# Four routing passes in place of six over streamed weights, with one buffer of normed rows and a front paced by TensorE time

## The chip, the cores and the metric

One core of a Trainium2 chip runs the whole program. Its engines are TensorE (PE: matmuls, PEld: weight loads), VectorE (DVE), ScalarE (ACT), GpSimd (POOL) and SyncE (SP, which here only issues DMAs); 16 DMA engines move data between HBM and the on-chip memory. The metric is the time of one execution in microseconds (us); lower is better.

## The reference, cut to what matters

One layer of a streaming encoder for 1024 prompt rows and 32 sample rows of width 1024, in float32. After two mixers (a gated linear attention and a forgetting attention, "fox", whose keys and values come partly from a cache) each row picks single-neuron experts by product keys and adds their outputs:

```python
def peer(h, w_q, subkeys, u_tab, v_tab):        # h: (rows, 1024)
    q = (xb @ w_q).reshape(blk, PEER_HEADS, 2, PEER_DKEY // 2)          # 8 heads, 2 halves of 128
    s = jnp.einsum('nhcd,hckd->nhck', q, subkeys)                       # 128 scores per half
    s1, i1 = lax.top_k(s[:, :, 0], 16)
    s2, i2 = lax.top_k(s[:, :, 1], 16)
    cand = (s1[..., :, None] + s2[..., None, :]).reshape(blk, 8, 256)
    top, ti = lax.top_k(cand, 16)
    idx = e1 * 128 + e2                                                 # one of 16384 experts
    g = jax.nn.softmax(top, axis=-1)
    a = jax.nn.gelu(jnp.einsum('nhkd,nd->nhk', u_tab[idx], xb))
    return jnp.einsum('nhk,nhkd->nd', g * a, v_tab[idx])
...
x = x + concat[GLA, FoX] @ w_out
x = x + peer(rmsnorm(x, g_norm2), ...)
```

So each row needs 8 heads x 16 = 128 experts, each with a row of `u` and a row of `v` (4 KB + 4 KB).

## The kernel before, in words

Rows are worked on in tiles of 128: tiles 0 to 7 are the prompt, tile 8 (`TILES`) holds four copies of the 32 sample rows, so that its 128 experts per row take only 32 gathers. The first phase (`mix_phase`, not touched) computes the projections and the linear attention of all tiles. The second, `merged_phase`, is written as two streams that every engine interleaves in the same order:

- the **back** goes through NS = 1056 slots. In slot s GpSimd gathers one expert per row, 128 rows of 8 KB (`u` and `v` together), into a ring of 8 buffers (L983). VectorE forms the dot products of the `u` half with the normed rows `h2` (L1493). A pair of slots makes a group: ScalarE applies the gelu to its two columns (L1102), VectorE multiplies by the routing weights (L1485), and the two `v` halves are added up. An add runs either on TensorE, as two matmuls of 512 columns with a diagonal matrix that ScalarE builds (L1110, L1295; the trace has four records for one add), or on VectorE as one instruction on `sums` (L1501). `on_vector(g)` says how many of a group's two adds VectorE takes: 1 in every odd group, 0 in every even group, so every fourth add. A ring buffer is free for the next gather when its add is done. At the start of a tile `reopen` (L1467) computes `h2` of the tile anew from x_mid rows that GpSimd's queue has loaded into `sums`.
- the **front** does, tile by tile, what the gathers need: `attend` (33 steps: keys and queries turned, then per head scores on TensorE, row maximum on VectorE L1325, exponential on ScalarE L1019, turn and use of the probabilities), `project` (w_out in 4 chunks of 1 MB, residual add L1348, norm, turn) and `route`. `route` goes through units; a unit is one head of one tile and has `UNIT` = 16 steps: at its step 0 TensorE does 16 matmul records of key scores into PSUM (L1270), at step 2 ScalarE copies them out (L1079), from step 4 on VectorE finds the best 16 of each half and of their sums and builds indexes and weights (24 instructions, L1379 to L1443), at step 13 ScalarE does the softmax's exponential (L1085).

`BATCHES` says which tiles share one pass over the streamed weights: a batch loads the 4 chunks of w_out and the 8 chunks of folded key weights (`keys_w`) once, 12 MB. There are six: [0], [1], [2, 3], [4, 5], [6, 7], [8]. All chunks pass through three buffers on the SP queue (`chunk`, L933), behind the loads of keys, queries, mixed rows and x rows (`rows`).

How the streams are interleaved is planned on the host by `front_plan`. Each front step has a weight (2 in attention and output, 1 in routing) and each unit and each batch has a due slot; from these it computes `PROLOGUE`, the front steps done before slot 0 (77), and `UPTO[s]`, the steps that must be done by slot s. `drive` runs slot s of the back and then the front up to `UPTO[s]`, on every engine alike. VectorE, ScalarE and TensorE each take their instructions in this one order, so an instruction that waits holds up all that is behind it on its engine.

Of the kernel before, what the change touches and what calls it, by code (L numbers as in the profile page):

```python
# [612 lines left out]
BATCHES = [[0], [1], [2, 3], [4, 5], [6, 7], [8]]  # L613
NB = max(len(ts) for ts in BATCHES)
PLACE = {t: (bi, i) for bi, ts in enumerate(BATCHES) for i, t in enumerate(ts)}
CW = 2 * DKEY
OUT_CH = D // CW
CHUNKS = OUT_CH + PH
# [13 lines left out]
def units_before(bi):  # L632
    return PH * sum(len(ts) for ts in BATCHES[:bi])


def cols_before(bi):
    return OUT_CH * sum(len(ts) for ts in BATCHES[:bi])

# [32 lines left out]
def mix_fill(t):
    return fills_before(t) + 2 + FH * quads(t)


def h2_fill(t):
    bi, i = PLACE[t]
    last = BATCHES[bi][-1]
    return mix_fill(last) + 2 + 2 * i
# [6 lines left out]
def unit_of(t, j):  # L685
    bi, i = PLACE[t]
    return units_before(bi) + j * len(BATCHES[bi]) + i
# [6 lines left out]
def front_plan():  # L694

    weight, due = [], []
    for ts in BATCHES:
        weight += [2] * (ATT_STEPS * len(ts) + out_steps(ts))
        base = len(weight)
        due += [(base, SLOTS * t - 12) for t in ts if t]  # L700
        weight += [1] * route_steps(ts)
        per_head = len(ts)
        for i, t in enumerate(ts):
            for j in range(PH):
                m = j * per_head + i
                due.append((base + UNIT * m + CHAIN_AT + 14, SLOTS * t + slots_of(t) // PH * j))
# [18 lines left out]
PROLOGUE, UPTO, FRONT = front_plan()  # L725


def on_vector(g):

    if GRP * g >= SLOTS * TILES:  # L730
        return 0
    return g % 2
# [15 lines left out]
def merged_phase(nc, ctx, io, dram):  # L748
# [32 lines left out]
    xT = [sb(f"rows_T{i}", [P, KD, P]) for i in range(NB)]  # L781
# [9 lines left out]
    cand = sb("candidates", [P, TOPK, TOPK])  # L791
    cand2 = sb("candidates_rest", [P, TOPK, TOPK])
# [3 lines left out]
    hot = sb("expert_pair_one_hot", [P, 2, TOPK, TOPK])  # L796
    pick = sb("expert_pair_keys", [P, 2, TOPK])
# [4 lines left out]
    IDX = 4  # L802
# [7 lines left out]
    h2 = sb("h2_rows", [P, 2, D])  # L810
    sums = sb("v_sums", [P, 2, D])
    folded = [sums[:].rearrange("p b n -> p (b n)"), h2[:].rearrange("p b n -> p (b n)")]
# [72 lines left out]
    def _(sp):  # L885
# [5 lines left out]
        def rows(t):  # L891
            bi, i = PLACE[t]
            b = t % 2
# [4 lines left out]
            sp.dma_start(qr[:], dram["q"][t]).then_inc(kq_in, 16)  # L898
            if t >= 2:
                sp.wait_ge(q_t, h2_fill(t - 2) + 2)  # L900
            sp.dma_start(mix[b][:, 0:GH * GV], dram["mixg"][t]).then_inc(mixg_in[b], 16)
            if bi:
                sp.wait_ge(p_h2, BATCHES[bi - 1][-1] + 1)
                sp.wait_ge(xm_st, 16 * (BATCHES[bi - 1][-1] + 1))
            sp.dma_start(xr[i][:], dram["xr"][t]).then_inc(xr_in[i], 16)
# [13 lines left out]
        def chunk(bi, c):  # L919
            n = CHUNKS * bi + c  # L920
            b = n % WBUF
            if n == 2:
                sp.wait_ge(f_mm, 4 * PH)
            if n >= WBUF:
                bu, cu = divmod(n - WBUF, CHUNKS)
                tiles = len(BATCHES[bu])
                if cu < OUT_CH:
                    sp.wait_ge(y_mm, cols_before(bu) + (cu + 1) * tiles)
                else:
                    sp.wait_ge(s_mm, units_before(bu) + (cu - OUT_CH + 1) * tiles)  # L930
            if c >= OUT_CH and bi == 0:
                sp.wait_ge(f_st[(c - OUT_CH) % 2], 16 * ((c - OUT_CH) // 2 + 1))
            sp.dma_start(wb[b][:], dram["w_out"][c] if c < OUT_CH else dram["keys_w"][c - OUT_CH]).then_inc(wb_in[b], 16)  # L933

        for bi, ts in enumerate(BATCHES):
            for t in ts:
                rows(t)
                if t == TILES:
                    past()
            if bi == 0:  # L940
                sp.dma_start(wb[2][:], dram["subkeys_T"].rearrange("p a k -> p (a k)")).then_inc(sub_in, 16)
                for h in range(PH):
                    sp.dma_start(ring[:, h, :], dram["w_qT"][h]).then_inc(wq_in[h], 16)
                    if h == 0:
                        sp.dma_start(v[:, 0:TILES, :], io["p_fox_v"].rearrange("(n p) c -> p n c", p=P)).then_inc(kv_in, 16)
                    if h < 2:
                        chunk(0, h)
            for c in range(2 if bi == 0 else 0, 7):
                chunk(bi, c)
            sp.wait_ge(xm_r, cols_before(bi + 1))  # L950
            for t in ts:
                sp.dma_start(dram["xm"][t], xr[PLACE[t][1]][:]).then_inc(xm_st, 16)
            for c in range(7, CHUNKS):
                chunk(bi, c)
# [646 lines left out]
```

## Time and profile before

| | |
|---|---|
| median of 3 runs | 3928.57 us (3922.43 to 3935.04) |
| profiled execution | 3929.12 us |
| its span, first to last instruction | 3927.5 us |
| mean granted TensorE clock | 0.88 of full speed |
| first dot product of the back (slot 0) | 902.2 us |
| moved by DMA in all | 1267.87 MB |

A busy share is an average over stages of different kinds. The page's slices show where the kinds change; the view of windows gives each engine's busy time, the granted clock, the DMA share and the rate in GB/s for a stretch; the view of waits says for whom an engine stood idle and for how long in all. "Slot" below always means a gather of the back, counted by the records of L1493 (each has a second record that reads its accumulator, so that view counts two per slot).

### The profile page before, as it was taken

What the parts mean: (1) busy time and instruction counts of PE and PEld (TensorE: products, weight loads), DVE (VectorE), ACT (ScalarE), POOL (GpSimd) and SP (SyncE); (2) the same over time, 40 slices, a digit from 0 to 9 for tenths busy, and PEclk for the clock granted to TensorE, in tenths of its full rate; (3) what the DMA queues carried; (4) which work ended last, traced back from release to release, by engine and by line L of the source; (5) the groups of instructions that cost most, each with busy time, mean ns of one, the idle gap of its engine ahead of it and who ended that gap; (6) DMA issues with size and microseconds to landing.
All of it is one profiled execution on the core that took longest, in us unless ns stands there. A gap on an engine that the chain in (4) does not pass through costs nothing.

```text
span 3927.5 us, 33430 instructions
## 1 busy us (share of the span) xinstructions
PE 3116.0 (79%) x9089; PEld 1656.2 (42%) x9089; DVE 2581.0 (66%) x6288; ACT 1163.9 (30%) x2530; POOL 1308.2 (33%) x1145
## 2 busy tenths in 40 slices
PE   5999999776786788777789777798877778866767
PEld 3665556463343335333345333344533333532322
DVE  2432334228768766898765898865698776577874
ACT  1222232212432343222353322344222223322211
POOL 0000000003444433444443444433344443344443
PEclk9778877778898899988899988899998889988889
DMA  3010000089999999999999999998999998899998
GB/s 160 25 41 22 22 24 26 17 309 377 412 420 415 404 403 376 420 413 406 401 397 362 400 418 401 396 379 317 401 418 414 399 415 348 349 420 416 410 417 347
DMA packets 187364, 1267.87 MB, mean 323 GB/s; under 512 B 23381, under 2 KB 24238, under 8 KB 39606
## 3 DMA queue, kind: packets, MB, share of 16 engines
q0 software_dynamic: 159488, 1131.10, 71.1%
q1 hardware_dynamic: 25350, 122.09, 7.9%
q10 hardware_dynamic: 2352, 12.72, 0.8%
q8 instruction: 65, 1.06, 0.1%
q14 instruction: 109, 0.89, 0.1%
HBM read 1238.95 MB, written 26.88 MB: 322 GB/s over the span
## 4 chain that ended last, share of the span: by engine, by line
PE 33%; DMA 21%; DVE 13%; issue 7%; ACT 5%; POOL 1%; DVEq 0%; SPq 0%; ACTq 0%; POOLq 0%
PE ps_acc L1295 21%; DMA uv_ring<-in_peer_uv,expert_index 20%; DVE uv_ring L1493 5%; PE ps_scores L1270 4%; PE ps_scores L1238 3%; DVE v_sums L1501 2%; PE ps_scores L1151 2%; ACT coef_diag L1110 2%; PE ps_fox_o L1169 1%; DVE key_top_index L1383 1%; PE ps_turn L1162 1%; DVE key_scores_rest L1384 1%; ACT L1019 1%; PE ps_acc L1139 1%; PE ps_scores L1152 1%
## 5 line engine op out<-in xcount | busy, mean ns | idle before, releaser
L1295 PE MATMUL ps_acc<-uv_ring,coef_diag 128*128 128x512 f32 x3200 | 1736.0, 690 | 680.1 <-ACT coef_diag L1110 679.7
L983 POOL DMA_INDIRECT uv_ring<-in_peer_uv,expert_index x1056 | 1260.5, 1194 | 1756.9 <-PE ps_acc L1295 1623.1
L1493 DVE CUSTOM_DVE_ANT_0 uv_ring<-uv_ring,h_rows 128x1024 f32<-128x1024 f32 x1056 | 1286.9, 1221 | 309.5 <-DMA uv_ring<-in_peer_uv,expert_index 306.0
L1295 PEld LDWEIGHTS ps_acc<-uv_ring,coef_diag 128*128 128x128 f32 x3200 | 663.6, 219 | 1618.6 <-ACT coef_diag L1110 924.8
L1102 ACT ACTIVATE gelu_u_dot_h<-u_dot_h 128x2 f32<-128x2 f32 x528 | 107.3, 203 | 1370.2 <-DVE u_dot_h L1493 1368.7
L389 PE MATMUL ps_z<-w_in,x_T 128*128 128x512 f32 x864 | 397.6, 619 | 0.0
L1110 ACT ACTIVATE coef_diag<-ident_f,coefficients 128x128 f32<-128x128 f32 x768 | 279.1, 395 | 332.0 <-DVE coefficients L1485 331.6
L1501 DVE SCALAR_TENSOR_TENSOR v_sums<-uv_ring,coefficients,v_sums 128x1024 f32<-128x1024 f32 x256 | 327.6, 1280 | 0.0
L1270 PE MATMUL ps_scores<-weight_chunk,rows_T 128*128 128x256 f32 x1152 | 261.9, 381 | 0.7 <-issue 0.7
L389 PEld LDWEIGHTS ps_z<-w_in,x_T 128*128 128x128 f32 x864 | 169.2, 200 | 206.6 <-issue 206.6
L1270 PEld LDWEIGHTS ps_scores<-weight_chunk,rows_T 128*128 128x128 f32 x1152 | 220.1, 191 | 61.0 <-issue 34.3
L1102 ACT ACT_TABLE_LOAD x143 | 183.5, 1283 | 2.5
L1325 DVE TENSOR_REDUCE neg_max<-ps_scores 128x1 f32<-128x128 f32 (+8 forms) x72 | 58.4, 811 | 168.9 <-PE ps_scores L1154 168.7
L1485 DVE TENSOR_TENSOR coefficients<-gelu_u_dot_h,expert_weight 128x2 f32<-128x2 f32 x528 | 81.0, 154 | 105.5 <-ACT gelu_u_dot_h L1102 104.7
L1238 PE MATMUL ps_scores<-weight_chunk,rows_T 128*128 128x256 f32 x576 | 127.6, 379 | 1.5 <-issue 0.8
L1238 PEld LDWEIGHTS ps_scores<-weight_chunk,rows_T 128*128 128x128 f32 x576 | 109.2, 190 | 24.3 <-issue 9.1
L1029 ACT ACTIVATE prob_T<-ps_turn 128x512 f32<-128x512 f32 (+3 forms) x112 | 53.0, 502 | 223.5 <-PE ps_turn L1162 220.3
L1151 PE MATMUL ps_scores<-k_pairs_T,q_pairs_T 64*128 64x512 f32 (+4 forms) x240 | 112.0, 548 | 0.0
L1169 PEld LDWEIGHTS ps_fox_o<-v_rows,prob_T 128*128 128x128 f32 x720 | 92.2, 193 | 32.0 <-issue 31.2
L483 DVE COPY gate_logits<-ps_gate_ds 128x256 f32<-128x256 f32 x9 | 3.8, 425 | 150.1 <-PE ps_gate_ds L401 150.1
L432 PE MATMUL ps_q_T_level<-level_q,level_k 64*128 64x128 f32 x280 | 68.3, 419 | 32.3 <-DVE level_k L531 32.3
L1085 ACT ACT_TABLE_LOAD x71 | 91.1, 1283 | 1.2
(206 smaller groups left out, 2648.0 us busy)
## 6 DMA issues: line engine op xcount, KB each, us to landing
weight_chunk<-scratch_keys_w SPq DMA_DIRECT2D x48, 1024.0 KB, 9.1
weight_chunk<-in_w_out_chunks SPq DMA_DIRECT2D x24, 1024.0 KB, 13.3
uv_ring<-in_peer_uv,expert_index POOLq DMA_INDIRECT x1056, 11.8
w_in<-in_w_in SPq DMA_DIRECT2D x8, 1548.0 KB, 24.6
uv_ring<-in_w_peer_q_T SPq DMA_DIRECT2D x8, 1024.0 KB, 22.7
x_T<-in_x_T POOLq DMA_DIRECT2D x9, 512.0 KB, 3.8
x_rows<-in_x_rows POOLq DMA_DIRECT2D x9, 512.0 KB, 4.6
x_mid<-in_x_rows SPq DMA_DIRECT2D x9, 512.0 KB, 16.3
```

The source lines that it names most:

```text
L389: m = pe.matmul(Z[c % 2][:, 0:n], xT[b][:, k, :], w[:, k, off:off + n], start=(k == 0), stop=(k == KD - 1))
L983: pool.indirect_dma_start(out=ring[:, s % RING, :], out_offset=None, in_=dram["uv"], in_offset=bass.IndirectOffsetOnAxis(ap=idx[:, t % IDX ...
L1085: act.activation(pe_[:], tv[:], ACT.Exp, bias=nmx[:], accum_out=psum_[:]).then_inc(tex, 1)
L1102: act.activation(gel[:, g % 2, :], dots[:, g % 2, :], ACT.Gelu).then_inc(geld, 1)
L1110: act.activation(diag[:, (GRP * g + n) % RING, :], matrix[:], ACT.Copy, scale=coef[:, g % 2, n:n + 1]).then_inc(dgd, 1)
L1151: pe.matmul(S[:, lo + x:lo + y], qT[a:a + FD, pair, :], kT[a:a + FD, pair, x:y], start=True, stop=False)
L1169: mm = pe.matmul(O[:, h, :], pT[k % 2][0:blocks[n], n - 4 * q, :], v[0:blocks[n], n, h * FD:(h + 1) * FD], start=(n == 0), stop=(n == len( ...
L1238: mm = pe.matmul(S[:, 512 * (step % 3):512 * (step % 3) + CW], xT[i][:, k, :], wb[chunk % WBUF][:, k * CW:(k + 1) * CW], start=(k == 0), s ...
L1270: mm = pe.matmul(S[:, 512 * (m % 3):512 * (m % 3) + CW], xT[i][:, k, :], wb[chunk % WBUF][:, k * CW:(k + 1) * CW], start=(k == 0), stop=(k ...
L1295: mm = pe.matmul(acc[:, c, :], diag[:, r, :], ring[:, r, D + c * 512:D + (c + 1) * 512], start=first, stop=False, skip_group_check=True)
L1493: dve.tensor_tensor_reduce(out=ring[:, s % RING, 0:D], in0=ring[:, s % RING, 0:D], in1=h2[:, t % 2, :], scale=1.0, scalar=0.0, op0=ALU.mul ...
L1501: dve.scalar_tensor_tensor(out=sums[:, b, :], in0=ring[:, (GRP * g + x) % RING, D:], scalar=coef[:, g % 2, x:x + 1], in1=sums[:, b, :], op ...
```

## The change

`BATCHES` becomes a list of batches of groups: [[0]], [[1, 2]], [[3, 4, 5]], [[6, 7], [8]]. A group goes through w_out together, a batch through the key weights together. `chunk_order` writes the order of the chunks out. Weights of the plan become fractions, one kind for attention by tile, one for output and one for routing, and `at_work` no longer rounds a slot's work up to whole steps. `BESIDE` tells which slots have attention or output beside them; there `on_vector` gives VectorE one add of every group. `h2` has one buffer, so `reopen` waits for all dot products of the tile before and stands at a tile's first slot. `cand` and `cand2` lie over `hot`, `IDX` is 5, and `folded[1]` lies over `rows_T`. The SP queue's order is written anew by groups.

```diff
-BATCHES = [[0], [1], [2, 3], [4, 5], [6, 7], [8]]
+BATCHES = [[[0]], [[1, 2]], [[3, 4, 5]], [[6, 7], [8]]]
+FLAT = [[t for ts in groups for t in ts] for groups in BATCHES]
+GROUPS = [ts for groups in BATCHES for ts in groups]
...
+def chunk_order():
+    order, out_at, keys_at = [], [], []
+    for bi, groups in enumerate(BATCHES):
+        for _ in groups:
+            gi = len(out_at)
+            out_at.append(len(order))
+            order += [("out", gi, c) for c in range(OUT_CH)]
+        keys_at.append(len(order))
+        order += [("keys", bi, j) for j in range(PH)]
+    return order, out_at, keys_at
...
 def front_plan():
-    weight, due = [], []
-    for ts in BATCHES:
-        weight += [2] * (ATT_STEPS * len(ts) + out_steps(ts))
+    weight, due, on_pe = [], [], []
+    for groups in BATCHES:
+        for ts in groups:
+            for t in ts:
+                weight += [(13.0 + 7.5 * min(t, TILES - 0.5)) / ATT_STEPS] * ATT_STEPS
+            weight += [3.5] * (OUT_CH * len(ts)) + [1.5] * (out_steps(ts) - OUT_CH * len(ts))
+            due += [(len(weight), SLOTS * t - 24) for t in ts if t]
         base = len(weight)
-        due += [(base, SLOTS * t - 12) for t in ts if t]
-        weight += [1] * route_steps(ts)
+        on_pe += [True] * (base - len(on_pe))
+        tiles = [t for ts in groups for t in ts]
+        weight += [0.45] * route_steps(tiles)
+        on_pe += [False] * route_steps(tiles)
...
-    upto, f = [], first
+    upto, at_work = [], total[first]
     for s in range(NS):
-        ahead = [(total[g] - total[f]) / (at - margin - s) for g, at in due if at - margin > s and g > f]
-        goal = total[f] + (max(ahead) if ahead else len(weight))
-        g = f
-        while g < len(weight) and total[g] < goal:
-            g += 1
-        f = g
-        upto.append(f)
-    return first, upto, len(weight)
+        ahead = [(total[g] - at_work) / (at - margin - s) for g, at in due if at - margin > s and total[g] > at_work]
+        at_work += max(ahead) if ahead else total[-1]
+        upto.append(max(f for f in range(len(total)) if total[f] <= at_work + 1e-6))
+    beside = [f < len(on_pe) and on_pe[f] for f in upto]
+    return first, upto, len(weight), beside
...
-    return g % 2
+    return 1 if BESIDE[GRP * g + GRP] else g % 2
...
+    cand, cand2 = hot[:, 0], hot[:, 1]
-    IDX = 4
+    IDX = 5
-    h2 = sb("h2_rows", [P, 2, D])
+    h2 = sb("h2_rows", [P, D])
...
                 for n in range(loaded, OUT_AT[gi] + WBUF):
+                    chunk(n)
+                for t in after:
+                    keys_queries(t)
+                    x_rows(t)
+                if TILES in after:
+                    past()
+                loaded = max(loaded, OUT_AT[gi] + WBUF)
+                for n in range(loaded, OUT_AT[gi] + OUT_CH + WBUF):
+                    chunk(n)
+                loaded = OUT_AT[gi] + OUT_CH + WBUF
+                sp.wait_ge(xm_r, cols_before(gi + 1))
+                for t in ts:
+                    sp.dma_start(dram["xm"][t], xr[PLACE[t][1]][:]).then_inc(xm_st, 16)
+                for t in after:
+                    mix_rows(t)
...
+            wait(dve, dotted, SLOTS * t)
...
-                if s == 0:
-                    reopen(0)
-                if i == SLOTS - 4 and t < TILES:
-                    reopen(t + 1)
+                if i == 0 and s < NS:
+                    reopen(t)
```

## Rows read from the trace of the kernel before

**Rows 1.** Page, busy us (share) xinstructions, and GB/s in 40 slices
```profile
PE 3116.0 (79%) x9089; PEld 1656.2 (42%) x9089; DVE 2581.0 (66%) x6288; ACT 1163.9 (30%) x2530; POOL 1308.2 (33%) x1145
...
GB/s 160 25 41 22 22 24 26 17 309 377 412 420 415 404 403 376 420 413 406 401 397 362 400 418 401 396 379 317 401 418 414 399 415 348 349 420 416 410 417 347
```

**Rows 2.** Windows: stretch, length, busy (x) PE PEld DVE ACT POOL, clock, DMA share, GB/s
```profile
902.20:3927.50 3025.30, 2353.51 (x6464) 1165.71 (x6464) 2263.95 (x5548) 946.36 (x2134) 1257.72 (x1057) 0.90 0.98 396
902.20:1027.10 124.90, 86.60 (x195) 41.93 (x196) 108.23 (x323) 34.24 (x80) 45.81 (x38) 0.83 0.98 395
...
2180.80:2537.60 356.80, 269.58 (x656) 131.00 (x654) 322.76 (x921) 101.35 (x244) 165.25 (x132) 0.90 1.00 407
2638.10:2746.40 108.30, 98.21 (x359) 49.71 (x358) 62.49 (x105) 51.79 (x93) 38.63 (x34) 0.92 0.85 328
3271.00:3386.00 115.00, 107.53 (x413) 57.52 (x412) 62.55 (x101) 54.24 (x100) 35.50 (x33) 0.93 0.78 297
3768.70:3835.70 67.00, 44.85 (x81) 17.22 (x82) 42.52 (x73) 10.31 (x34) 31.37 (x28) 0.87 1.01 419
3835.70:3927.50 91.80, 66.40 (x132) 25.79 (x130) 45.61 (x85) 14.34 (x48) 26.36 (x26) 0.93 0.83 342
```

**Rows 3.** Windows of L1493 alone (two records a slot): VectorE busy, clock, share, GB/s
```profile
2180.80:2537.60 356.80, 159.35 (x260) 0.90 1.00 407
...
3768.70:3835.70 67.00, 32.07 (x52) 0.87 1.01 419
```

**Rows 4.** Waits of VectorE, 2180.8 to 2537.6 (total us, times, longest)
```profile
DVE key_top L1379 <- ACT key_scores L1079: 17.1, 14, 2.9
DVE uv_ring L1493 <- DMA uv_ring<-in_peer_uv,expert_index: 9.6, 11, 2.0
DVE coefficients L1485 <- ACT gelu_u_dot_h L1102: 4.6, 17, 0.3
```

**Rows 5.** Waits of VectorE, 3271.0 to 3386.0 (attention of tile 8)
```profile
DVE neg_max L1325 <- PE ps_scores L1154: 26.9, 6, 7.5
DVE coefficients L1485 <- ACT gelu_u_dot_h L1102: 23.4, 12, 5.1
```

**Rows 6.** Timeline 2290 to 2298, a unit's chain behind one add
```profile
2290.04 0.14 DVE L1485 TENSOR_TENSOR coefficients<-gelu_u_dot_h,expert_weight 128x2 f32<-128x2 f32 x1
...
2293.19 3.62 PE L1270 MATMUL ps_scores<-weight_chunk,rows_T 128*128 128x256 f32 x16
...
2296.84 0.38 ACT L1079 ACTIVATE key_scores<-ps_scores 128x256 f32<-128x256 f32 x1 [1.89 <-PE ps_scores L1270]
...
2297.26 0.49 DVE L1379 MAX8 key_top<-key_scores 128x8 f32<-128x128 f32 x2 [0.89 <-ACT key_scores L1079]
```

**Rows 7.** Timeline 994 to 1010, a unit's chain behind two adds
```profile
996.19 0.19 DVE L1485 TENSOR_TENSOR coefficients<-gelu_u_dot_h,expert_weight 128x2 f32<-128x2 f32 x1
...
997.86 6.53 PE L1295 MATMUL ps_acc<-uv_ring,coef_diag 128*128 128x512 f32 x8 [4.55 <-ACT coef_diag L1110]
...
1004.23 3.62 PE L1270 MATMUL ps_scores<-weight_chunk,rows_T 128*128 128x256 f32 x16
...
1008.29 0.49 DVE L1379 MAX8 key_top<-key_scores 128x8 f32<-128x128 f32 x2 [3.45 <-ACT key_scores L1079]
```

**Rows 8.** Waits of VectorE, 902.2 to 1027.1 (the others there: 0.8 us)
```profile
DVE key_top L1379 <- ACT key_scores L1079: 14.6, 4, 7.6
```

**Rows 9.** Page, DMA issues: count, KB each, median us to landing
```profile
weight_chunk<-scratch_keys_w SPq DMA_DIRECT2D x48, 1024.0 KB, 9.1
weight_chunk<-in_w_out_chunks SPq DMA_DIRECT2D x24, 1024.0 KB, 13.3
```

**Rows 10.** Page, costliest groups: VectorE's adds
```profile
L1501 DVE SCALAR_TENSOR_TENSOR v_sums<-uv_ring,coefficients,v_sums 128x1024 f32<-128x1024 f32 x256 | 327.6, 1280 | 0.0
```

**Rows 11.** Waits of VectorE, 1027.1 to 1109.3 (attention of tile 1)
```profile
DVE neg_max L1325 <- PE ps_scores L1154: 10.0, 5, 5.1
```

**Rows 12.** Timeline of TensorE, 2284 to 2314, two adds after a short gap
```profile
2297.57 3.70 PE L1295 MATMUL ps_acc<-uv_ring,coef_diag 128*128 128x512 f32 x8 [0.76 <-ACT coef_diag L1110]
```

More of the change, by code:

```diff
@@ L924, in chunk @@
             if n >= WBUF:
[L925 to L928, printed above, removed]
-                else:
[L930 to L939, printed above, removed]
+                was, owner, part = CHUNK_ORDER[n - WBUF]
+                if was == "out":
+                    sp.wait_ge(y_mm, cols_before(owner) + (part + 1) * len(GROUPS[owner]))
+                else:
+                    sp.wait_ge(s_mm, units_before(owner) + (part + 1) * len(FLAT[owner]))
+            if kind == "keys" and at == 0:
+                sp.wait_ge(f_st[c % 2], 16 * (c // 2 + 1))
+            sp.dma_start(wb[b][:], dram["w_out"][c] if kind == "out" else dram["keys_w"][c]).then_inc(wb_in[b], 16)
+        loaded = 0
+        for bi, groups in enumerate(BATCHES):
+            for t in groups[0]:
+                keys_queries(t)
+                mix_rows(t)
+                x_rows(t)
+            if TILES in groups[0]:
+                past()
             if bi == 0:
@@ L946, in _ @@
                     if h < 2:
[L947 to L954, printed above, removed]
+                        chunk(h)
+                loaded = 2
+            for k, ts in enumerate(groups):
+                gi = GROUP[ts[0]]
+                after = groups[k + 1] if k + 1 < len(groups) else []
+                for n in range(loaded, OUT_AT[gi] + WBUF):
+                    chunk(n)
+                for t in after:
+                    keys_queries(t)
+                    x_rows(t)
+                if TILES in after:
+                    past()
+                loaded = max(loaded, OUT_AT[gi] + WBUF)
[3 more added lines that the diff above has]
+                sp.wait_ge(xm_r, cols_before(gi + 1))
+                for t in ts:
+                    sp.dma_start(dram["xm"][t], xr[PLACE[t][1]][:]).then_inc(xm_st, 16)
+                for t in after:
+                    mix_rows(t)
+            for n in range(loaded, KEYS_AT[bi] + PH):
+                chunk(n)
+            loaded = KEYS_AT[bi] + PH
     @block.gpsimd
@@ L1088, in front @@
         def front():
-            for bi, ts in enumerate(BATCHES):
-                for t in ts:
-                    yield from attend(t)
-                yield from project(bi, ts)
-                yield from route(bi, ts)
+            for bi, groups in enumerate(BATCHES):
+                for ts in groups:
+                    for t in ts:
+                        yield from attend(t)
+                    yield from project(GROUP[ts[0]], ts)
+                yield from route(bi, FLAT[bi])
         def back():
@@ L1342, in project @@
                     c, i = divmod(step - 1, n)
-                    dve.wait_ge(y_mm, cols_before(bi) + step)
+                    dve.wait_ge(y_mm, cols_before(gi) + step)
+                    bi, place = PLACE[ts[i]]
                     if c == 0:
-                        dve.wait_ge(xr_in[i], 16 * sum(len(us) > i for us in BATCHES[:bi + 1]))
-                    half = xr[i][:, c * CW:(c + 1) * CW]
+                        dve.wait_ge(xr_in[place], 16 * sum(len(us) > place for us in FLAT[:bi + 1]))
+                    half = xr[place][:, c * CW:(c + 1) * CW]
                     bank = 512 * ((step - 1) % 3)
```

153 lines of the change are left out of this document (82 added, 71 removed).

## The prediction

> **What bounds the kernel now.** I read the page's busy shares and its forty slices first [rows 1]: no engine is near its whole span, but from about 900 us on the DMA line stands at 400 GB/s and above. So the program has two parts. Up to 902.2 us run the mixing phase and the prologue; the change leaves their work as it is. From 902.2 us, the first dot product of L1493, 1056 gathers of 1.049 MB follow one another; I call one gather a slot, and slot s is record s+1 of L1493. The slices say "DMA", yet a busy share hides who waits, so I cut this part by the plan's stages (view of windows, [rows 2]) and looked at what VectorE waited for in each.
>
> Three kinds of stretch come out. In the last free slots, with no front work, a slot takes 67.0 / 26 = 2.58 us at 419 GB/s with VectorE 63% busy [rows 2, 3]: bytes bind. In attention of late tiles TensorE is 91 to 94% busy and the rate falls to 328 and 297 GB/s, 3.3 and 3.5 us a slot: TensorE and the turns around it bind, and VectorE there waits for scores and for the gelu [rows 2, 5]. In a routing stretch (2180.8 to 2537.6, 130 slots, 2.745 us each) the DMA share reads 1.00, but VectorE is busy 322.8 of 356.8 us, and of its 34 us idle only 9.6 are a wait for a gather; 17.1 are a wait for the key scores [rows 2, 4]. The row to learn from is this one: a DMA share of 1.00 stands there beside an engine that is at its own limit. In 902.2 to 1027.1 VectorE waits for no gather at all, only for key scores [rows 8], and still the share reads 0.98.
>
> **Bytes.** The passes go from six to four and the w_out groups from six to five: 48 + 24 chunks [rows 9] become 32 + 20, 20 fewer of 1.049 MB. 396 GB/s over 3025.3 us are 1198 MB [rows 2]; 21 fewer leave 1177. At 418 GB/s (419 in the free row, 416 to 422 in other stretches where VectorE waits for gathers) they are worth 50 us, but only where bytes bind.
>
> A page of the Trainium skill speaks against any such rate: "DMA: Bandwidth & Descriptors", section "Where 436 GB/s comes from", has the HBM side of a core bind near 358 GB/s. The row shows 419 here, so the measurement decides. By the page the bytes-bound stretches below would take some 200 us more, and I give that no weight.
>
> **Adds.** `on_vector` now puts one add per pair of gathers on VectorE wherever the plan has TensorE front work beside it. Counted from the plan, VectorE does 369 adds in place of 256. 113 more at 1.28 us [rows 10] are 145 us of VectorE and as many adds of about 1.9 us less on TensorE. They all fall into attention and output stretches, where a slot then costs VectorE about 1.9 us and its share of attention (a late tile: 62.6 us in 33 slots less 33 x 1.64, so 9 us): hidden under 2.78 us of bytes. If a gather's bytes came faster than that the adds would still have 0.5 us a slot of room.
>
> **Pace.** This is the part that decides. I worked `front_plan` out for both versions. Before, routing runs at 2 steps a slot, so one unit (one head of one tile, 16 steps) per 8 slots; attention at 1 step a slot, whatever it costs TensorE. After, steps are weighed by TensorE time: attention of tile 7 spreads over 56 slots and of tile 8 over 61 (33 each before), and in exchange a routing unit gets 5 slots (slots 4 to 30), 6.1 (92 to 190, and 348 to 497) and 6.45 (726 to 867). After slot 868 only two units are left. A unit is cheap for TensorE and dear for VectorE, and the weights don't see VectorE.
>
> Price on VectorE. A gather with every fourth add: 42.52 / 26 = 1.635 us [rows 2, 3], and 0.035 of gelu wait (4.6 / 130, [rows 4]): 1.67. A unit: (322.76 - 130 x 1.635) / 16 = 6.9 us. Then the wait for the key scores. Its chain: coefficients, diagonal, the pair's adds on TensorE, 16 score matmuls (3.62 us), copy, key_top. Behind one add it is 2297.26 - 2290.04 = 7.2 us [rows 6], which is also the median of the 57 such units in the timeline. Behind two adds it is 12.1 us [rows 7]; the twelve such units lie between 9.8 and 12.8, and I take 11: TensorE had idled 4.55 us and did the 8 matmuls in 6.53 us at the lower of its clocks (1.2 GHz), against 3.70 for 8 after a short gap [rows 12]. Before, VectorE reaches key_top two slots later, and 8 slots a unit keep the pairing fixed, nearly always the short chain: 17.1 / 16 = 1.07 us a unit [rows 4]. After, 6.1 slots a unit run through all cases. Of the 62 dense units 31 fall behind one add, and VectorE has 5.0 to 8.3 us of own work meanwhile: waits of 2.2 (6 units: even slot, one slot on), 0.95 (10), 0.2 (7), 0 (8), mean 0.8. 31 fall behind two: 7.2 (6), 4.7 (9), 3.9 (10), 2.3 (6), mean 4.5. Both: 2.6 us a unit. The five units in slots 4 to 30: 3.2. The only such run in the trace has 14.6 us in 4 waits [rows 8]. The ends for this unknown are 0.9 (today's phase) and 4.5.
>
> **The sum.** Dense routing, each as slots x 1.67 + units x (6.9 + wait): slots 0 to 30, 10 + 45 + 37 + 17 = 109; 92 to 190, 165 + 110 + 42 = 317; 348 to 497, 250 + 166 + 62 = 478; 726 to 867, 237 + 152 + 57 = 446. Together 1350 us for 422 slots, 3.2 us each; bytes alone would ask about 2.65.
> Attention and output, 446 slots: 467.7 MB of gathers, 26 MB of chunks, 10 of rows, 4 of the cache, 8 of x_mid out and in: about 516 MB at 418 GB/s = 1234 us. Slots 31 to 64 hold attention of tiles 1 and 2 at 2.4 and 1.65 steps a slot; there TensorE asks about 2.4 us a slot and a head's row maximum waited up to 5.1 us even at 1 step a slot [rows 11]: 20 us more, of bounds 0 and 80 (16 heads x 5.1).
> Free slots: 156 x 2.577 = 402, and the last 32 as now, 91.8 [rows 2]: 494.
> 1350 + 1254 + 494 = 3098, with 902.2 before it 4000.3 of span, and 1.6 us around it (3929.12 against 3927.5) 4002. The profiled execution is 0.55 us above the median, so no correction. As a balance: now the slots take 3025 - 1198 / 0.418 = 159 us more than their bytes ask, of which attention of tiles 7 and 8 has 23 and 33 ([rows 2], length less GB/s x length / 418). After, that excess is 3098 - 1177 / 0.418 = 282: the stalls of attention go, and 422 slots at 0.55 us over their bytes come.
>
> **Edits at nothing.** One `h2` buffer in place of two: `reopen` costs its 1.28 us as before but now sits between the last dot product of a tile and the first of the next; the eight-deep ring covers that, and its x_mid was asked for 20 slots earlier; without cover 9 x 1.3. `cand` laid over `hot` and one memset less: same instructions, waits that `ready()` had already. `IDX` 5: tile 5's routing needs only tile 0's sums done and stands in tile 2's and 3's slots, so nothing waits. On the SP queue `mix_rows` of the second group now comes behind the x_mid stores, and in the last batch keys, x rows and the 4.2 MB of `past()` stand ahead of the fourth output chunk of tiles 6 and 7; that chunk then lands behind some 5 MB, 12 us at the whole rate and 25 at half of it, and is wanted only three quarters into an output stage of 34 slots (90 us); if it came late TensorE would stand at it, with the adds of the back behind it, some 10 us once. The POOL queue keeps its order.
>
> **Rivals.** (1) The two-add chain stays warm: with 6 slots a unit TensorE idles less before the pair, so 8 matmuls take 3.70 and the chain 8.3 us. Waits behind two adds fall to 1.8, the mean to 1.3: -81 and -10, 3911. For it: TensorE's work per slot rises from 2.07 to about 2.2 us; against: the slot grows too, and in the last routing stretch of before all eight chains run behind two adds and take 10.2 to 12.8 us. The page "TensorE: Matmul & The Clock Gate" of the Trainium skill, section "What's actually happening", says the array is at 1.2 GHz unless it is kept busy; by its rule the cold pair after an idle wait stays, which is what the 6.53 us row shows, and the sum stays 4002. (2) The phase matters little and a unit waits 0.9 as today: -1.7 x 62 - 2.3 x 5.4 = -118, 3884. For it: 53 of the 69 units after slot 0 are in that phase now, and it is the only one seen often. (3) The spread does what its name says and bytes bind everywhere: 902.2 + 1177 / 0.418 + 10 + 1.6 = 3730. Against it: VectorE alone, without any wait for scores, asks 1.67 x 6.1 + 6.9 = 17.1 us a unit, 2.8 a slot. (4) Worse still: the dense attention in slots 31 to 64 stalls as the late tiles do now, each head's maximum 5 us: 4062.
>
> **How the numbers follow.** Forecast 0.50, between 3960 and 4045; the rival of the warm pair 0.20, 3890 to 3940; today's wait 0.14, 3860 to 3917; bytes everywhere or halfway there 0.06, under 3860; more than 4045, 0.10. A measurement tells 0.3% (12 us) from no change. Faster takes the third and fourth case and half of the second: 0.30; within 0.3%: 0.10; slower 0.60. The range 3870 to 4050 leaves out the fourth case and most of the last. As most of the chance lies in cases of both signs: the forecast's own range is 3960 to 4045.
>
> **What would show it.** In the windows of slots 92 to 190 and 348 to 497: VectorE's busy time near 2.76 us a slot, 3.1 to 3.2 us a slot in all, key_top's wait for key scores 35 to 50 us in the first and 50 to 75 in the second, waits for gathers near none, the rate near 350 GB/s. In attention of tiles 6 to 8: 410 GB/s or more, 2.8 us a slot, TensorE near 75% busy. The weight chunks 32 and 20. First dot product at 902 us. I am wrong at the root if VectorE waits for gathers in the dense stretches, wrong in size if a unit's wait is 1 us.

## The result, and the profile after

The changed kernel is slower: 3990.11 us median (3989.63 to 3992.23) against 3927.07 for the kernel before in the same comparison, a ratio of 1.0156 with a 95% interval of 1.0139 to 1.0173. The forecast was 4002. The profiled execution took 3990.19 us with a span of 3988.6, and the first dot product came at 905.0.

The page of the kernel after: busy us (share) xinstructions of each engine, the rate in 40 slices, and the lines that answer to [rows 1, 9, 10], with the group of the key scores' first use.

```profile
PE 2991.5 (75%) x8637; PEld 1591.5 (40%) x8637; DVE 2734.9 (69%) x6400; ACT 1124.1 (28%) x2411; POOL 1271.1 (32%) x1145
...
GB/s 158 24 40 22 21 24 32 42 305 363 330 421 369 361 354 396 419 377 414 395 356 364 330 339 380 414 391 416 416 397 410 354 346 364 341 404 420 420 419 354
...
L1564 DVE SCALAR_TENSOR_TENSOR v_sums<-uv_ring,coefficients,v_sums 128x1024 f32<-128x1024 f32 x369 | 472.3, 1280 | 0.0
...
L1442 DVE MAX8 key_top<-key_scores 128x8 f32<-128x128 f32 x144 | 35.0, 284 | 148.7 <-ACT key_scores L1140 148.7
...
weight_chunk<-scratch_keys_w SPq DMA_DIRECT2D x32, 1024.0 KB, 7.9
weight_chunk<-in_w_out_chunks SPq DMA_DIRECT2D x20, 1024.0 KB, 17.4
```

Two things moved as the diff says: 20 chunks fewer (DMA moved 1246.83 MB in all, before 1267.87), and 369 adds on VectorE. The slices already show the shape: plateaus of 330 to 370 GB/s where long stretches of routing run (the 13th to 15th, 21st to 24th and 32nd to 35th), and mostly 390 to 420 in the other slices after the 11th. Before, the dips were few and belonged to attention [rows 1].

Windows of the kernel after (length, busy us (x) of PE PEld DVE ACT POOL, granted clock, DMA share, GB/s), cut by the plan's stages. In order: all gathers; routing of slots 0 to 30; attention of tiles 1 and 2; routing of slots 92 to 190; attention and output up to slot 347; routing of slots 348 to 497; attention and output of tiles 6 to 8, and in it attention of tile 7 (59 slots) and of tile 8 (62 slots); routing of slots 726 to 867; free slots; the last 32.

```profile
905.00:3988.60 3083.60, 2229.31 (x6012) 1102.00 (x6012) 2418.04 (x5661) 906.56 (x2015) 1220.58 (x1057) 0.87 0.96 382
905.00:1011.00 106.00, 69.62 (x167) 35.76 (x168) 94.16 (x296) 30.91 (x67) 30.09 (x29) 0.84 0.92 361
1011.00:1060.10 49.10, 38.43 (x118) 19.15 (x117) 29.48 (x53) 27.70 (x52) 14.70 (x14) 0.78 0.91 366
1060.10:1120.80 60.70, 46.98 (x170) 23.92 (x168) 43.12 (x75) 35.48 (x65) 24.30 (x21) 0.87 0.86 334
...
1197.70:1513.20 315.50, 223.64 (x550) 112.27 (x551) 277.67 (x836) 88.25 (x203) 116.45 (x100) 0.87 0.93 360
1513.20:1944.70 431.50, 329.31 (x1083) 173.81 (x1081) 323.78 (x524) 164.88 (x326) 186.11 (x158) 0.88 0.99 407
1944.70:2426.60 481.90, 341.37 (x832) 171.04 (x832) 415.71 (x1256) 133.44 (x308) 172.96 (x154) 0.87 0.91 347
2426.60:3060.50 633.90, 475.96 (x1488) 240.40 (x1488) 471.75 (x740) 204.04 (x414) 258.42 (x230) 0.85 1.00 409
2566.80:2732.60 165.80, 128.75 (x384) 60.43 (x384) 121.72 (x187) 57.62 (x111) 68.48 (x60) 0.81 0.99 400
2841.10:3002.00 160.90, 130.66 (x438) 64.20 (x436) 126.99 (x197) 61.43 (x122) 68.86 (x62) 0.88 0.99 403
3060.50:3503.70 443.20, 316.87 (x779) 158.43 (x780) 394.21 (x1206) 124.52 (x289) 172.53 (x143) 0.89 0.92 356
3503.70:3899.90 396.20, 265.57 (x502) 105.45 (x500) 265.66 (x499) 64.97 (x206) 185.32 (x160) 0.88 1.01 415
3899.90:3988.60 88.70, 62.62 (x132) 24.35 (x132) 48.24 (x96) 14.71 (x49) 27.55 (x26) 0.97 0.85 348
```

Read the seventh against the stretch of before in [rows 2]: VectorE is busy 415.7 of 481.9 us, and the rate is 347 GB/s where 407 stood. What ends most of VectorE's other 66 us is in its waits there (total us, times, longest):

```profile
DVE key_top L1442 <- ACT key_scores L1140: 56.8, 16, 7.7
DVE coefficients L1548 <- ACT gelu_u_dot_h L1164: 1.7, 8, 0.3
DVE uv_ring L1556 <- DMA uv_ring<-in_peer_uv,expert_index: 1.2, 2, 0.8
```

In 150 slots VectorE waits only 1.2 us for gathers. The transfers are ready; VectorE comes late, and the ring's buffers come free late. One such wait from close by, in the timeline of the kernel after, 2218 to 2232 (start, duration, engine, operation, idle before it), answers to [rows 7]:

```profile
2218.38 1.28 ACT L1146 ACT_TABLE_LOAD   x1
2218.93 0.15 DVE L1548 TENSOR_TENSOR coefficients<-gelu_u_dot_h,expert_weight 128x2 f32<-128x2 f32 x1
...
2219.98 0.68 ACT L1172 ACTIVATE coef_diag<-ident_f,coefficients 128x128 f32<-128x128 f32 x2
...
2220.42 6.55 PE L1358 MATMUL ps_acc<-uv_ring,coef_diag 128*128 128x512 f32 x8 [5.14 <-ACT coef_diag L1172]
...
2226.81 3.62 PE L1332 MATMUL ps_scores<-weight_chunk,rows_T 128*128 128x256 f32 x16
...
2230.46 0.38 ACT L1140 ACTIVATE key_scores<-ps_scores 128x256 f32<-128x256 f32 x1 [7.07 <-PE ps_scores L1332]
...
2230.88 0.49 DVE L1442 MAX8 key_top<-key_scores 128x8 f32<-128x128 f32 x2 [7.72 <-ACT key_scores L1140]
```

From the coefficients to key_top 11.95 us. The unit's exponential (table load at 2218.38) stands ahead of the diagonals on ScalarE and costs them about 1 us. TensorE had idled 5.14 us and did its 8 matmuls in 6.55 us, at the lower of its two clocks (1.2 GHz). VectorE had 4.2 us of own work behind the coefficients and then stood for 7.72.

### The profile page after: what moved, and what is told of

Read it like the earlier page. It is cut to its first block and busy times, and to the rows that moved or that the text cites. A ratio compares the mean times of both kernels' runs of the same rounds, so it can differ in the third digit from the quotient of the medians.

```text
span 3988.6 us, 32600 instructions
## 1 busy us (share of the span) xinstructions
PE 2991.5 (75%) x8637; PEld 1591.5 (40%) x8637; DVE 2734.9 (69%) x6400; ACT 1124.1 (28%) x2411; POOL 1271.1 (32%) x1145
## 2 busy tenths in 40 slices
DMA packets 184481, 1246.83 MB, mean 313 GB/s; under 512 B 23062, under 2 KB 23919, under 8 KB 39287
## 5 line engine op out<-in xcount | busy, mean ns | idle before, releaser
L1358 PE MATMUL ps_acc<-uv_ring,coef_diag 128*128 128x512 f32 x2748 | 1584.1, 719 | 848.3 <-ACT coef_diag L1172 847.8
L1044 POOL DMA_INDIRECT uv_ring<-in_peer_uv,expert_index x1056 | 1223.4, 1158 | 1858.8 <-PE ps_acc L1358 1661.2
L1358 PEld LDWEIGHTS ps_acc<-uv_ring,coef_diag 128*128 128x128 f32 x2748 | 577.2, 225 | 1675.1 <-ACT coef_diag L1172 1119.3
L1564 DVE SCALAR_TENSOR_TENSOR v_sums<-uv_ring,coefficients,v_sums 128x1024 f32<-128x1024 f32 x369 | 472.3, 1280 | 0.0
L1172 ACT ACTIVATE coef_diag<-ident_f,coefficients 128x128 f32<-128x128 f32 x655 | 246.1, 396 | 278.6 <-DVE coefficients L1548 278.4
L1332 PE MATMUL ps_scores<-weight_chunk,rows_T 128*128 128x256 f32 x1152 | 265.6, 385 | 0.7 <-issue 0.7
L1442 DVE MAX8 key_top<-key_scores 128x8 f32<-128x128 f32 x144 | 35.0, 284 | 148.7 <-ACT key_scores L1140 148.7
L1300 PE MATMUL ps_scores<-weight_chunk,rows_T 128*128 128x256 f32 x576 | 132.7, 385 | 1.1 <-issue 0.8
L1213 PE MATMUL ps_scores<-k_pairs_T,q_pairs_T 64*128 64x512 f32 (+4 forms) x240 | 120.6, 585 | 1.3 <-ACT q_pairs_T L1068 0.7
L1231 PE MATMUL ps_fox_o<-v_rows,prob_T 128*128 128x64 f32 x720 | 95.0, 279 | 4.6 <-ACT prob_T L1090 4.6
```

The source lines that it names most:

```text
L1044: pool.indirect_dma_start(out=ring[:, s % RING, :], out_offset=None, in_=dram["uv"], in_offset=bass.IndirectOffsetOnAxis(ap=idx[:, t % IDX ...
L1172: act.activation(diag[:, (GRP * g + n) % RING, :], matrix[:], ACT.Copy, scale=coef[:, g % 2, n:n + 1]).then_inc(dgd, 1)
L1213: pe.matmul(S[:, lo + x:lo + y], qT[a:a + FD, pair, :], kT[a:a + FD, pair, x:y], start=True, stop=False)
L1231: mm = pe.matmul(O[:, h, :], pT[k % 2][0:blocks[n], n - 4 * q, :], v[0:blocks[n], n, h * FD:(h + 1) * FD], start=(n == 0), stop=(n == len( ...
L1300: mm = pe.matmul(S[:, 512 * (step % 3):512 * (step % 3) + CW], xT[PLACE[ts[i]][1]][:, k, :], wb[chunk % WBUF][:, k * CW:(k + 1) * CW], sta ...
L1332: mm = pe.matmul(S[:, 512 * (m % 3):512 * (m % 3) + CW], xT[i][:, k, :], wb[chunk % WBUF][:, k * CW:(k + 1) * CW], start=(k == 0), stop=(k ...
```

## The experiments

My theory: the loss is routing packed so densely that VectorE, not the bytes, sets the slot (its instructions, then the key-score wait), while attention and output gained what was forecast. Rivals: the adds moved to VectorE cost the time; the pace is at fault, and a looser one brings it back; the saved passes are worth nothing. All ratios are against the kernel before, with 95% intervals.

**undo_adds**: the moved adds taken back.

```diff
-    return 1 if BESIDE[GRP * g + GRP] else g % 2
+    return g % 2
```

> on_vector is g % 2 again, so VectorE does 256 adds as before the change; all else as changed. My theory (routing units too dense for VectorE, each waiting for key scores behind TensorE's adds) says VectorE has slack in attention and output, so taking 113 adds of 1.28 us off it gains nothing there, while TensorE gets 113 adds back: 3990 to 4030 us, dense routing windows unchanged at 315, 482 and 443 us. The rival, that the moved adds are the loss, says 113 x 1.28 us come back: about 3870 us.

4012.26 us (4007.01 to 4016.78), ratio 1.0215 (1.0173 to 1.0256): 22 us worse. The routing of tiles 3 to 5 stayed as it was (slots 348 to 498, 484.8 against 484.3 us). Attention of tile 1 went from 3.5 to 4.2 us a slot and of tile 8 from 2.60 to 2.84, but tile 7 became faster, over the same 59 slots. Its attention in undo_adds:

```profile
2583.80:2744.30 160.50, 134.42 (x442) 64.92 (x441) 104.42 (x173) 62.30 (x127) 72.16 (x60) 0.95 1.02 417
```

TensorE did 442 records in place of 384, at a clock of 0.95 in place of 0.81. So the moved adds help on balance and are not the cause of the loss.

**early4**: the unit's key scores stay where they are on TensorE, and ScalarE's copy and VectorE's routing steps come four steps later, so that four steps more lie between issue and use, without another buffer.

```diff
-CHAIN_AT, EXP_AT = 4, 13
+CHAIN_AT, EXP_AT = 8, 17
...
-    return UNIT * PH * len(ts) + 4
+    return UNIT * PH * len(ts) + CHAIN_AT
...
-                m, r = divmod(step - 2, UNIT)
+                m, r = divmod(step - (CHAIN_AT - 2), UNIT)
```

> The changed kernel with ScalarE's copy, its exponential and VectorE's routing steps each 4 steps later than TensorE's key scores (copy at step 6, key_top at step 8, exponential at 17), so that scores have some 1.5 slots more time; nothing else moves. My theory says key_top's wait of 149 us in all falls under 20 and the three dense stretches shrink by nearly all of it, to VectorE's busy time: 3850 to 3880 us. The rival, that the wait only hides another limit (ring turnaround, bytes), says the idle time moves to another line: 3960 to 3990 us.

3885.57 us (3873.21 to 3889.34), ratio 0.9883 (0.984 to 0.9925): 104 us better than the change alone, and 6 us above the expected range. key_top's wait after slot 0 fell from 138.3 to 15.3 us. The stretch of tiles 3 to 5 in early4, slots 348 to 498 (151 slots; 484.3 us in the kernel after) as in the next two, and VectorE's waits there:

```profile
1922.70:2358.00 435.30, 321.86 (x835) 166.02 (x836) 418.17 (x1259) 133.40 (x309) 177.12 (x154) 0.92 0.97 386
```

```profile
DVE uv_ring L1556 <- DMA uv_ring<-in_peer_uv,expert_index: 3.8, 4, 1.3
DVE key_top L1442 <- ACT key_scores L1140: 3.8, 6, 1.5
```

VectorE is now 96% busy with the same 418 us of work as in the kernel after: the wait went, the work stayed. That is VectorE's own bound, close to the 2.88 us that a slot takes here.

**pe_only**: in routing stretches, and in the free slots behind them, VectorE takes no add, which changes the formula's 1.67 us a slot and leaves the wait.

```diff
-    return 1 if BESIDE[GRP * g + GRP] else g % 2
+    return 1 if BESIDE[GRP * g + GRP] else 0
```

> The changed kernel with no add on VectorE in routing stretches and no shift (key scores as close to key_top as in the changed kernel). A second point for my formula: VectorE asks 1.35 a slot and 6.9 a unit; every chain now runs behind two adds, but TensorE is busier and warm, so 8.4 us, against 3.9 to 7.1 of VectorE's own work: waits of about 2.9 us a unit. 6.1 x 1.35 + 6.9 + 2.9 = 18.0 us a unit, 2.96 a slot, so 390 slots gain 0.24 us: 3880 to 3910 us, with key_top's wait about as large as in the changed kernel or larger. If the chain goes cold behind two adds (11 us) the waits are 5 us a unit and it gives 3990 or more. If VectorE's busy time alone decides, it comes out like the kernel with the shift, 3815.

3916.03 us (3907.19 to 3920.01), ratio 0.9969 (0.9953 to 0.9985), 6 us above the expected range. The three long routing stretches took 1161 us, 2.96 a slot, as expected. In pe_only, the same stretch and its wait:

```profile
1929.10:2376.80 447.70, 366.73 (x992) 186.11 (x991) 373.43 (x1221) 146.11 (x348) 176.35 (x153) 0.98 0.96 375
```

```profile
DVE key_top L1442 <- ACT key_scores L1140: 61.8, 21, 7.2
```

Every pair now has two adds on TensorE, and yet the chain was shorter than 11 us: 8.2 was its most frequent length, and the mean over the 62 units of the three stretches was 9.0. The clock of the stretch was 0.98 in place of 0.87, and mostly 8 matmuls took 3.70 us even after some idle time. In 11 of the 62 units they took 5.4 to 6.4 us, at times after an idle time that was no longer. Two rows of its TensorE timeline:

```profile
2023.54 5.40 PE L1358 MATMUL ps_acc<-uv_ring,coef_diag 128*128 128x512 f32 x8 [2.19 <-ACT coef_diag L1172]
...
2043.51 3.70 PE L1358 MATMUL ps_acc<-uv_ring,coef_diag 128*128 128x512 f32 x8 [2.58 <-ACT coef_diag L1172]
```

So the mean wait was 2.5 us a unit (2.9 expected), against 2.07 in the kernel after.

**early4_pe**: both edits together.

> early4 and, in routing stretches, no add on VectorE at all (TensorE does both adds of every group there). My theory: VectorE, busy 2.78 us a slot in the dense stretches, loses 0.32 of it, so bytes (2.65) bind there and 390 slots gain 0.2 us each: about 3815 us, between 3790 and 3850. The rival: TensorE, which then asks 1 add of 1.9 to 2.2 us and 0.6 of scores in each slot, becomes the bound: 3880 or more, with the wait for key scores back.

3814.91 us (3812.88 to 3819.1), ratio 0.9722 (0.9706 to 0.9739). It beats both kernels, and is 175 us better than the change; the two edits alone give 104 and 74, so they nearly add up. The stretch in early4_pe:

```profile
1893.00:2301.20 408.20, 358.78 (x991) 186.91 (x992) 374.88 (x1221) 144.84 (x347) 180.18 (x154) 0.98 1.01 411
```

```profile
DVE uv_ring L1556 <- DMA uv_ring<-in_peer_uv,expert_index: 18.7, 23, 2.4
DVE key_top L1442 <- ACT key_scores L1140: 4.0, 5, 2.0
```

For the first time in such a stretch of the changed kernel the gathers are what VectorE waits for most, at 411 GB/s: the bytes bind.

**w75, early4_w75, old_pace**: a looser pace for routing, by its weight (w75), with the shift of early4 beside it, or with all old weights and due times.

```diff
-        weight += [0.45] * route_steps(tiles)
+        weight += [0.75] * route_steps(tiles)
```

> The changed kernel with the plan's weight of a routing step 0.75 in place of 0.45: a unit gets 7.2 to 8.3 slots in place of 6.1 to 6.45, attention of tile 7 gets 45 slots in place of 59 and of tile 8 48. My theory: dense routing is 526 slots x 1.67 + 69 units x 8.9 = 1490 us, attention and output 342 slots of about 407 MB at 418 GB/s = 973 us, free slots 485: about 3865 us, between 3850 and 3910. The rival that fewer passes or the moved adds are the loss says no change from 3990; the rival that late attention would stall again at 45 slots a tile says 3950 or more.

> Both edits. My theory: with no wait for key scores a unit of 7.2 slots asks 1.67 x 7.2 + 6.9 = 18.9 us of VectorE, 2.63 a slot, about what its bytes ask, so that bytes bind nearly everywhere: 3750 to 3800 us, rate near 410 GB/s in all windows after 905 us. The rival that the two edits cure the same time says no more than the better of the two alone, about 3860 us.

```diff
-                weight += [(13.0 + 7.5 * min(t, TILES - 0.5)) / ATT_STEPS] * ATT_STEPS
-            weight += [3.5] * (OUT_CH * len(ts)) + [1.5] * (out_steps(ts) - OUT_CH * len(ts))
-            due += [(len(weight), SLOTS * t - 24) for t in ts if t]
+                weight += [2] * ATT_STEPS
+            weight += [2] * out_steps(ts)
+            due += [(len(weight), SLOTS * t - 12) for t in ts if t]
...
-        weight += [0.45] * route_steps(tiles)
+        weight += [1] * route_steps(tiles)
```

> The changed kernel with the old weights (2 a step in attention and output, 1 in routing) and the old due slots; four passes, the adds rule, one h2 buffer stay. A unit gets 7.2 to 9.7 slots, late attention 39. My theory (density of routing against VectorE is the loss; its formula slots x 1.67 + units x 8.9 for the dense part gives 1525 us): 3940 to 3965 us. If four passes or the adds were the loss it stays at 3990; if the new weights alone were, it falls well under the kernel before, to 3880 or less.

w75: 3943.21 us, ratio 1.0042 (1.0025 to 1.0059), a miss: 78 above the expected 3865 and 33 above its range. early4_w75: 3865.57, ratio 0.9834 (0.9793 to 0.9875), a miss by 66 from its range; the number fits the rival that I had put beside it (about 3860), though it is 20 better than early4 alone. old_pace: 3949.83, ratio 1.0056 (1.0036 to 1.0076), as expected. The routing side held: the formula gives 1490 us for w75's dense slots and 1525 for old_pace's, measured 1487 and 1531. What I had left out is attention. In w75 attention and output took 1050 us where their bytes ask 973. Attention of tile 2, squeezed into 18 slots, in w75 and then in early4_w75 with two waits of that window:

```profile
1066.10:1134.40 68.30, 56.77 (x165) 28.20 (x164) 37.80 (x65) 32.27 (x60) 18.10 (x18) 0.70 0.71 264
```

```profile
1061.00:1129.40 68.40, 56.87 (x165) 28.21 (x165) 37.91 (x66) 32.27 (x60) 18.09 (x18) 0.70 0.73 269
```

```profile
DVE neg_max L1387 <- PE ps_scores L1216: 25.5, 7, 6.2
...
POOL uv_ring L1044 <- PE ps_acc L1358: 51.9, 9, 10.1
```

3.8 us a slot: VectorE waits for scores, GpSimd for the adds behind them on TensorE, at a clock of 0.70. The change's own weights spare tile 2 this (2.9 us a slot) and so win back a part of what dense routing costs: old_pace, with its looser routing, is 40 us better than the change, no more. It is still 23 us slower than the kernel before, with 21 MB less to move. Its key_top waited 102.5 us after slot 0 where before had 57.8, and its units come every 7.2 to 9.7 slots in place of the fixed 8, but no run takes those 23 us apart.

**early4_flat and early4_pe_flat**: attention weighed more evenly over the tiles, once VectorE's wait is gone; early4_flat also has routing looser.

```diff
-                weight += [(13.0 + 7.5 * min(t, TILES - 0.5)) / ATT_STEPS] * ATT_STEPS
+                weight += [(36.0 + 4.0 * min(t, TILES - 0.5)) / ATT_STEPS] * ATT_STEPS
...
-        weight += [0.45] * route_steps(tiles)
+        weight += [0.65] * route_steps(tiles)
```

> early4 with a routing step weighted 0.65 and attention 36 + 4 t in place of 13 + 7.5 t: 6.6 slots a unit, tiles 1 and 2 get 20 and 22 slots in place of 14 and 21, tiles 6 to 8 46, 50 and 50. If early attention crowded into few slots is what early4_w75 lost to (1050 us in attention and output where bytes ask 973), this gives 3830 to 3855 us; if attention with VectorE's adds stalls at any pace near 30 to 45 slots a tile, it stays at 3865 to 3885.

3846.37 us, ratio 0.9789 (0.9766 to 0.9812), 39 better than early4, as expected. early4_pe_flat (early4_pe with 22.0 + 6.0 a tile):

> The same fastest kernel with attention weighted 22 + 6 t in place of 13 + 7.5 t, so that tile 1 gets 18 slots in place of 14 and tile 8 loses 4; the first routing stretch gets denser (4.5 slots a unit). Tile 1 stands at 3.4 us a slot where bytes ask 2.75, 9 us in all; I expect 3800 to 3820, a gain of at most 15 us. If attention is not what is left, no change.

3816.06 us, ratio 0.9708 (0.968 to 0.9735), which can't be told from early4_pe: with VectorE unloaded, this other spread gained nothing that a measurement shows.

**before_early4**: the shift of early4 in the kernel before.

> The kernel before with the same shift as early4 (copy at step 6, key_top at 8, exponential at 17). My theory: at 8 slots a unit the wait is 58 us in all after 902 us and a unit's slots are within 0.1 us of what their bytes ask, so at most half of it comes back: 3885 to 3910 us. The rival that the wait was harmless before (bytes bind there) says 3915 to 3930; the rival that the chain costs the two kernels alike says 3820.

3920.99 us, ratio 0.9989 (0.9975 to 1.0003): no change, a miss. key_top's wait fell from 57.8 to 3.6 us, but the waits for gathers rose from 306 to 368. Its routing window of 132 slots and the waits there:

```profile
2183.20:2539.10 355.90, 269.83 (x653) 134.76 (x652) 325.65 (x927) 101.69 (x247) 160.64 (x134) 0.88 1.00 411
```

```profile
DVE uv_ring L1493 <- DMA uv_ring<-in_peer_uv,expert_index: 19.9, 24, 2.2
DVE coefficients L1485 <- ACT gelu_u_dot_h L1102: 4.6, 17, 0.3
```

At 8 slots a unit the bytes stand ready right behind VectorE: of the 17.1 us of wait in [rows 4] most turned into waits for gathers (9.6 to 19.9), and the slot went from 2.745 to 2.696 us. So removing 54 us of this wait gained nothing measurable at the old pace, and removing 123 us of it gained 104 at the new one.

**six_passes**: early4_pe with the old six batches, to price the saved bytes where VectorE doesn't bind.

```diff
-BATCHES = [[[0]], [[1, 2]], [[3, 4, 5]], [[6, 7], [8]]]
+BATCHES = [[[0]], [[1]], [[2, 3]], [[4, 5]], [[6, 7]], [[8]]]
...
-NB = max(len(ts) for ts in FLAT)
+NB = 3
```

> The fastest kernel so far (shift of 4 steps, no routing adds on VectorE) with the six batches of before, one w_out group each. The weight stream is 21 MB longer. My theory: once VectorE is out of the way bytes bind nearly everywhere, so it takes 21 / 0.418 = 50 us more than 3815: 3850 to 3885 us. The rival that the passes were never worth anything says 3815 to 3825.

3850.02 us, ratio 0.9806 (0.9788 to 0.9824): beside the other edits the four passes are worth 35 us of the 50 that their bytes ask at 418 GB/s (the plan's stages move with the batches, so this is not the bytes alone). They move at 407 GB/s in six_passes and at 404 in early4_pe (all gathers of each):

```profile
900.00:3847.60 2947.60, 2335.86 (x6452) 1167.64 (x6452) 2291.31 (x5551) 938.51 (x2127) 1212.77 (x1057) 0.90 0.99 407
```

```profile
901.10:3813.20 2912.10, 2338.08 (x6600) 1175.75 (x6600) 2248.44 (x5514) 948.00 (x2162) 1237.79 (x1057) 0.92 0.99 404
```

**att_half**: early4_pe with the moved adds of attention back on TensorE.

```diff
-    return 1 if BESIDE[GRP * g + GRP] else g % 2
+    return g % 2 if BESIDE[GRP * g + GRP] else 0
```

> The same fastest kernel with every fourth add on VectorE in attention and output in place of every second, so TensorE has 113 adds more there. As with undo_adds, VectorE has slack there and TensorE less: 5 to 30 us slower than 3815, with the loss in tiles 1, 2 and 8 and the granted clock of those windows higher. If a warmer TensorE outweighs its longer queue, it is as fast or faster.

3832.23 us, ratio 0.9763 (0.9746 to 0.978): 17 us worse than early4_pe, as undo_adds was 22 worse. Attention of tile 1 in early4_pe and in att_half:

```profile
991.40:1039.10 47.70, 35.82 (x118) 18.14 (x117) 29.66 (x54) 27.56 (x52) 15.75 (x14) 0.82 0.98 395
```

```profile
990.80:1044.90 54.10, 42.23 (x137) 21.16 (x136) 26.00 (x52) 28.43 (x55) 14.83 (x14) 0.87 0.95 377
```

The gain sits in tiles 1, 2 and 8; in tile 7 there is none (2.78 against 2.76 us a slot); its clock was 0.83 with the adds moved and 0.92 with them back, which fits, but no run holds the clock fixed.

## Why the prediction came out

**Bytes: right.** 20 chunks fewer, 21.04 MB less moved; 382 GB/s over 3083.6 us are 1178 MB, forecast 1177. Worth 35 us where VectorE is out of the way (forecast 50); what they are worth in the changed kernel itself no run shows.

**Adds: right in size and place.** 369 of them, and attention and output of tiles 6 to 8 took 2.76 us a slot at 409 GB/s with TensorE 75% busy (forecast 2.8, 410, 75). Attention of tiles 7 and 8 alone took 2.81 and 2.60 us a slot, against 3.3 and 3.5 in [rows 2], where the looser spread has its part too. I had costed the adds at nothing and given their relief to TensorE in full; undo_adds and att_half show a net gain of 22 and 17 us. That the lower clock gave part of the relief back is argued from tile 7, not shown.

**Pace, VectorE's price: right.** VectorE was busy 2.805, 2.771 and 2.776 us a slot in the three long stretches (forecast 2.76), waited 0.8, 1.2 and 2.1 us for gathers in them (forecast near none), and the rates were 360, 347 and 356 GB/s (forecast 350). The formula, slots x 1.67 + units x (6.9 + wait), with a wait of 2.0 also gave w75's and old_pace's dense slots to 6 us, and with another price for a slot and another wait those of pe_only.

**Pace, the wait: right in kind, too large by a quarter.** 2.07 us a unit over the 62 dense units after slot 31, forecast 2.6; by stretch 32.1, 56.8 and 39.2 us (forecast 35 to 50 and 50 to 75 for the first two, so the first fell short). The classes came out in the forecast order. Behind two adds: 6.9, 3.8, 3.1 and 1.5 us (forecast 7.2, 4.7, 3.9, 2.3), with a chain of 10.9 us in the mean (forecast 11). Behind one: 2.0, 0, 0.1, 0 (forecast 2.2, 0.95, 0.2, 0). The chain was as forecast, so the mis-sized term is VectorE's own work between coefficients and key_top: behind two adds 7.2 us in the mean, where the forecast's 11 less 4.5 leaves 6.5.

**Luck in the total.** In the three long stretches this wait came to 128 us, 33 less than forecast. VectorE's busy time came out 20 us above the forecast (1088 us against 391 slots x 1.635 + 62 units x 6.9 = 1067), and its other idle time 11 us above (25 against 14). The two errors have opposite signs, and that these stretches hit their sum to 2 us is luck; the mechanism is right, and the terms are right to within a quarter, but for that small rest.

**The sum.** 106.0 + 315.5 + 481.9 + 443.2 = 1346.6 us of dense slots (forecast 1350), attention and output 1252.1 (1254), free and last slots 484.9 (494), and 905.0 (902.2) ahead of them. The excess over the bytes at 418 GB/s is 3083.6 - 2818 = 265 us (forecast 282).

The page "DMA: Bandwidth & Descriptors" of the Trainium skill, section "Where 436 GB/s comes from", has 358 GB/s as the limit of a core's HBM side, and beside it a measured 425. The free stretch of after moved 415, near the second figure and not the first, so here too the measurement decides; the prediction took the section to speak against any such rate, which is more than it says. Its "some 200 us more" is also low: by 358 GB/s the 1234 and 402 us of the forecast would grow by about 275 us, an estimate from that page's figure.

**Slots 31 to 64.** 109.8 us for 35 slots; 38.2 MB moved in them, 91.5 us at 418 GB/s, so 18 us over their bytes where I had taken 20. neg_max waited 5.5 us at most there: the fourth rival's price existed, but came to 15.7 us in six waits in tile 1 and 11.0 in tile 2, not at every head.

**Edits at nothing: no cost seen.** The nine `reopen` instructions took 1.28 us each, and only 0.2 us of any dot product waited on one. TensorE waited for no weight chunk in 2426.6 to 3060.5.

**The rivals.** The warm pair was false for the changed kernel (chain 10.9) and mostly true in pe_only (8.2 at its most frequent): I had the mechanism and not what turns it on. Today's wait, 0.9 us: refuted, 2.07. Bytes everywhere: refuted by the waits. At the change's own pace the gathers are what VectorE waits for most in all three long routing stretches only where both the wait and the adds are out of its way (early4_pe and att_half, at 409 to 411 GB/s). At a looser pace they are so in early4_w75 too, and in the last stretch of early4_flat and of old_pace. Why routing is slow in the changed kernel is shown by early4 (the wait, 104 us) and early4_pe (a further 71 with the adds out of VectorE's way). What stays open is the other 15 of the 50 us in six_passes: early4_pe has denser routing and a mean rate 3 GB/s lower, but no run took that apart.

## What to carry to other kernels

When one pacer spreads work over a bound stream, weigh each step by the engine that binds beside it, and by all of them: time per step on TensorE said nothing of the 6.9 us that a routing unit costs VectorE. When the pace changes, redo the interval between the step that issues a result and the step that reads it, for a wait that cost nothing measurable at one pace cost 104 us at the next, and went away by reading the scores four steps later. And judge a bound by who waits for whom: DMA shares of 0.91 to 0.93 stood beside a VectorE that waited at most 2.1 us for transfers in 316 to 482 us, and even 0.98 beside one that waited for none [rows 2, 8].

## What the runs showed of the hardware

- A DMA share is not a rate: 0.91 went with 347 GB/s, 1.00 with 407 and 409, 1.01 with 415.
- More work on TensorE can shorten a chain through it. With all routing adds there, its clock in the stretch rose from 0.87 to 0.98 and the chain behind two adds fell from 10.9 to 9.0 us in the mean, to 8.2 at its most frequent. The page "TensorE: Matmul & The Clock Gate" of the Trainium skill, section "What's actually happening", has the array at 1.2 GHz unless it is kept busy; the trace agrees in kind: 6.55 us for 8 matmuls after 5.14 us of idling, and 3.70 after 2.58 in a busier stretch. The idle time just before a group doesn't decide alone, for in that same stretch 8 took 5.40 us after 2.19.
- The reverse was seen too: with 58 matmul records fewer in tile 7's attention (59 slots in both kernels) the clock was 0.81 and not 0.95, TensorE's busy time only 128.8 us against 134.4, and the stretch longer (165.8 us against 160.5). It is one profiled execution of each kernel; early4_pe and att_half show the same in kind (clock 0.83 and 0.92, 2.78 and 2.76 us a slot).
